# Trainium2: moving head-projection units, output products, output stores and the final scaling in an eight-core hybrid conv/attention layer

## Chip, cores and metric

One Trainium2 chip (trn2), all 8 cores, each with its own share of the work and no traffic between them. The metric is device time in microseconds of the slowest core, from one launch.

## What is computed

```python
def hybrid_layer(x, ...):                       # x: (2, 4096, 4096) fp32
    proj = einsum('bsd,de->bse', rmsnorm(x, g_in), w_in)
    gB, gC, h, z_conv, c_q, c_kv, k_rope, z_attn = split(proj)   # 4x2048, 1024, 512, 64, 2048
    y_conv = gB * causal_short_conv(gC * h, conv_w) * silu(z_conv)
    q = rmsnorm(c_q) @ w_uq                     # 16 heads x (128 + 64 rotary)
    k_nope, v = split(rmsnorm(c_kv) @ w_ukv)    # 16 heads x (128 + 128)
    attn = chunk_causal_attention(rope(q), rope(k), v)           # chunks of 64 frames
    y = concat(y_conv, attn * silu(z_attn))
    return x + y @ w_out
out = rmsnorm(hybrid_layer(...), g_final)
```

## The kernel before

Each core owns 1024 query tokens (16 chunks of 64) of one sequence and computes everything for them; for the keys it projects all 4096 tokens of the sequence. All operands of TensorE are bf16. The program is written out instruction by instruction; `Prog` finds dependences from the addresses touched and turns them into semaphore waits. Every engine (PE, ACT, DVE, POOL, SP) runs its list strictly in the order written. At the end (`finish`, L163) each of the five engines waits for the last event of all engines and for every outstanding DMA. SP issues nearly all DMAs; POOL issues the ones that convert fp32 to bf16.

Stages in order of time:

- Convolution group (L429 to L672): projections in tiles of 128 channels; the last product of each tile f is stored to DRAM (`ysp`, L671).
- Latent keys (L756 to L792): 32 token tiles T. `post(T)` (L711) normalises and applies the rotary tables `cst` and the gain `gkv`, which SP loads at L756 to L758, behind the last `ysp` store.
- Query latents (L804): squares by ACT, summed over channels with a product with ones, which `pend` puts into the middle of the next tile (L813, L818).
- Attention (L1008): 16 heads h, each with query block b=0 (8 steps i of 256 keys) and b=1 (16 steps). A step issues the QK products of the next step (L946, L947), the exponential of its own (ACT, L1026), then perhaps one unit of projection work for the next head (Q: L882, K: L891, V: L900), the mask (DVE, L1045) and the products with V (L1052); DVE adds the exponentials up one step behind (L1059). The step's width is 512 queries; in the last 8 steps of a block it narrows from 512 to 64. `SKIP` names steps that take no unit. A unit needs a PSUM bank (`ubank`: bank 6 or 7) and is copied out in the next step, Q by DVE, K and V by ACT. A V unit covers 512 keys for two heads, so head 15's V comes with head 14's.
- Head 15 has no next head. It takes 8 pieces (`early`, four matmuls each) of the first output tile's product (L1001); the convolution results `YCV` and the weights `WO` for it are loaded when head 14's units are done (L1018 to L1022).
- Output (L1108): two groups g of four 128-token tiles, each 8 column tiles ct of 512, each 8 weight blocks kg (`WO`, 512 KB each, ten buffers, the load of block i+10 issued after block i's products). `evac` (L1087) adds the residual `XR` on DVE and squares on ACT. After group 0's last column tile `finish_tile` (L1094) scales all four tiles on DVE, 16 pieces of 1024 columns, and stores each; group 1 reuses the same `H` buffers. Group 1's last column tile is done tile by tile, with `finish_tile` after each.

Of the kernel before, what the change touches and what calls it, by code (L numbers as in the profile page):

```python
# [11 lines left out]
ALU = mybir.AluOpType  # L12
# [11 lines left out]
DMA_SEMS = {"sp": 40, "pool": 24}  # L24
# [60 lines left out]
class Prog:  # L85
# [77 lines left out]
    def finish(self):  # L163
# [6 lines left out]
        for e in ENGS:  # L170
            i = Ins(e, len(self.ins[e]), None, 0)
            i.deps = [x for x in evs if not (x.eng == e and x.dma_sem is None)]
            self.ins[e].append(i)
            self.order.append(i)
        known = {e: {} for e in ENGS}
        for ins in self.order:
            kn = known[ins.eng]
            todo = sorted(ins.deps, key=lambda x: -x.idx)
            for d in todo:
# [10 lines left out]
                kn[key] = val  # L190
            ins.known = dict(kn)
# [79 lines left out]
def build_program():  # L271
# [30 lines left out]
    with stack:  # L302
# [316 lines left out]

        wt = 2 * NF  # L620
# [183 lines left out]
        for m in range(8):  # L804
            w = WS[(64 + m) % 2]
            for hf in range(2):
# [142 lines left out]
        def finish_block(h, b_):  # L949
# [23 lines left out]
            [Z_Q + j * 4 * KB for j in range(4)] + [Z_R + 8 * KB, Z_R + 12 * KB, Z_R, Z_K2, Z_K2 + 4 * KB, Z_R + 4 * KB])]  # L973
# [8 lines left out]
        def woload(i):  # L982
# [7 lines left out]
            [Z_R + (16 + 2 * j) * KB for j in range(4)] + [Z_RB + 16 * KB + 512 + 2 * j * KB for j in range(4)])]  # L990
# [13 lines left out]
        SKIP = {(1, 1), (1, 3), (1, 5), (1, 7)}  # L1004
        qk(0)
        behind, slow, done = [], [], []
        us = []
        for n in range(len(steps)):  # L1008
            h, b_, i, off, w = geom(n)
            if b_ == 0 and i == 0:  # L1010
                us = []
                if h < 15:
                    us = units_of(h + 1)
                    pr = h // 2 + 1
                    if pr < 8:
                        us += [lambda s_=s_, pr=pr: unit_v(pr, s_) for s_ in range(8 * (h % 2), 8 * (h % 2) + 8)]
                else:
                    for i_ in range(6):  # L1018
                        woload(i_)
                    for f in range(16):  # L1020
                        dma("sp", YCV[:, f, :], ysp[f], [], [YCV[:, f, :], {("dr", "y", f)}])
                    load("sp", GF[:, :], gfin_d)  # L1022
# [5 lines left out]
            if us and (b_, i) not in SKIP:  # L1028
                us.pop(0)()
            if n % 6 == 0:  # L1030
                wcast(n // 6)
            if h == 15:
                pbanks[:] = [6]
                m_ = n - 360
                if m_ == 18:
                    woload(6)
                if 5 <= m_ < 9:
                    early.append((0, m_ - 5, 3))
                elif 14 <= m_ < 22 and m_ % 2 == 0:
                    early.append((0, m_ // 2 - 7, 2))  # L1040
                if early and early[-1] not in done:
                    done.append(early[-1])
                    out_mm(*early[-1][:2], early[-1][2], early[-1][1])
# [42 lines left out]

        def evac(g, ct, t_):  # L1087
            j = 32 * g + 4 * ct + t_
            h_ = H[t_][:, ct * 512:(ct + 1) * 512]
            tt(h_, bank(obank(ct, t_ + 4 * g)), XR[j % 8][:, :], ALU.add)  # L1090
            act(jk[:, :], h_, AF.Square, accum=fst[4 * g + t_][:, ct:ct + 1])  # L1091
            load_res(j + 8)

        def finish_tile(t_, pieces):  # L1094
            f_ = fst[t_]
            P.add("dve", lambda e: e.reduce_sum(out=f_[:, 8:9], in_=f_[:, 0:8], axis=AX.X), [f_[:, 0:8]], [f_[:, 8:9]])
            act(f_[:, 9:10], f_[:, 8:9], AF.Sqrt, scale=1.0 / D, bias=EPSA)
            recip(f_[:, 10:11], f_[:, 9:10])
            h_ = H[t_ % 4]
            n = D // pieces  # L1100
# [141 lines left out]
```

How the kernel before makes its waits and increments, by code:

```python
        def run(ename, eng):  # L207
            for i in self.ins[ename]:
                best = {}
                for d in i.waits:
                    key = d.dma_sem if d.dma_sem is not None else d.eng
                    val = d.dma_val if d.dma_sem is not None else d.ordinal
                    best[key] = max(best.get(key, 0), val)
                for key, val in best.items():
                    eng.wait_ge(dsem[key] if isinstance(key, tuple) else esem[key], val)
                if i.fn is None:
                    continue
                with nc.source_location(__file__, i.line):
                    r = i.fn(eng)
                if i.dma_sem is not None:
                    r.then_inc(dsem[i.dma_sem], 16)
                elif i.signal:
                    r.then_inc(esem[ename], 1)
```

The softmax here doesn't subtract the row's maximum and nothing guards it: scores larger than these inputs give would overflow.

## Time and profile before

| | |
|---|---|
| runs, us | 3679.06, 2735.65, 2737.66; median 2737.66 |
| profiled execution, us | 2735.57 |
| its span (slowest core, first to last instruction), us | 2734.0 |
| PE busy, us | 2671.2 (98% of the span) |
| DVE, ACT, POOL busy, us | 1419.5, 762.5, 79.2 |

Spans of all cores lie between 2726.2 and 2734.0 us. All views are of the slowest core, times in us from the start of its span. The profile shows a matmul from its start to a modelled end, so matmuls in a row overlap, and a short wait can vanish under the tail of the matmul before it.

### The profile page before, as it was taken

The page shows a single profiled execution, that of the slowest core. Times are in us where ns is not written, and L with a number is a line of the kernel's source. Part 1 is how long each engine was busy: PE and PEld are TensorE (multiplying, and loading weights), DVE is VectorE, ACT ScalarE, POOL GpSimd, SP SyncE. Part 2 cuts the span into 40 slices and gives each one's busy share as a digit, 9 for nine tenths or more (in the row PEclk, how much of TensorE's full clock was granted, in tenths as well). Part 3 has the DMA queues.
Part 4 walks back from the last instruction along what each step waited for, and adds up shares of the span by engine and source line. Part 5 has one row for each costly group of instructions (what it writes and reads, how often), then busy time and mean ns, then how long its engine had stood idle before and what let it go on. Part 6 is the DMA issues. An engine that isn't in the chain of part 4 may idle for free.

```text
span 2734.0 us, 41718 instructions; the slowest of 8 cores (2726.2 to 2734.0 us)
## 1 busy us (share of the span) xinstructions
PE 2671.2 (98%) x15646; PEld 1414.7 (52%) x15646; DVE 1419.5 (52%) x2314; ACT 762.5 (28%) x1187; POOL 79.2 (3%) x151
## 2 busy tenths in 40 slices
PE   6999999999999999999999999999999999998996
PEld 3446655555555555554444555555656544443443
DVE  3766765555555446664554257767676772013013
ACT  2300000000000026640110267666666661011011
POOL 0000000000000001100000000000000000000000
PEclk8999999999999999999999999999999999999998
DMA  9836666666666618855455544455435846568664
GB/s 216 206 103 161 162 170 174 169 171 178 180 171 167 133 32 138 134 134 160 125 176 152 101 72 56 71 78 70 63 47 78 101 147 213 187 187 247 230 194 167
DMA packets 122102, 390.87 MB, mean 143 GB/s; under 512 B 13616, under 2 KB 17968, under 8 KB 121776
## 3 DMA queue, kind: packets, MB, share of 16 engines
q1 hardware_dynamic: 97920, 308.24, 39.2%
q0 software_dynamic: 23984, 79.96, 20.1%
q8 instruction: 128, 2.10, 0.3%
q14 instruction: 70, 0.57, 0.1%
HBM read 447.13 MB, written 54.53 MB: 183 GB/s over the span
## 4 chain that ended last, share of the span: by engine, by line
PE 92%; DMA 3%; DVE 3%; issue 1%; ACT 1%; SPq 0%; DVEq 0%; ACTq 0%; POOLq 0%
PE ps L594 27%; PE ps L1001 14%; PE ps L832 8%; PE ps L702 7%; PE ps L1052 4%; PE ps L947 4%; PE ps L946 4%; PE ps L900 4%; PE ps L891 4%; PE ps L882 4%; PE ps L545 4%; PE ps L812 3%; PE ps L526 2%; PE ps L703 1%; DMA ust_90<-w_in_t 1%
## 5 line engine op out<-in xcount | busy, mean ns | idle before, releaser
L594 PE MATMUL ps<-XG,ws_67 128*128 128x384 bf16 (+2 forms) x2176 | 371.5, 332 | 0.0
L594 PE MATMUL ps<-XG,ws_66 128*128 128x384 bf16 (+2 forms) x2176 | 371.5, 332 | 0.0
L594 PEld LDWEIGHTS ps<-XG,ws_66 128*128 128x128 bf16 x2176 | 212.9, 98 | 154.5
L594 PEld LDWEIGHTS ps<-XG,ws_67 128*128 128x128 bf16 x2176 | 212.9, 98 | 154.3
L946 PE MATMUL ps<-QN_153,KH_149 128*128 128x512 bf16 (+7 forms) x384 | 115.2, 317 | 0.0
L946 PE MATMUL ps<-QN_154,KH_150 128*128 128x512 bf16 (+7 forms) x384 | 115.2, 317 | 0.0
L947 PE MATMUL ps<-TQ_156,K_61 128*128 128x512 bf16 (+7 forms) x384 | 115.2, 317 | 0.0
L947 PE MATMUL ps<-TQ_155,K_61 128*128 128x512 bf16 (+7 forms) x384 | 115.2, 317 | 0.0
L667 ACT ACTIVATE CC<-UU,convw 128x1024 f32<-128x1024 f32 x16 | 18.4, 1151 | 336.0 <-DVE UU L663 336.0
L832 PE MATMUL ps<-XG,ws_66 128*128 128x512 bf16 x512 | 112.0, 379 | 0.0
L832 PE MATMUL ps<-XG,ws_67 128*128 128x512 bf16 x512 | 111.8, 379 | 0.0
L1026 ACT ACTIVATE PT_157<-ps 128x1024 bf16<-128x1024 f32 x96 | 84.6, 882 | 66.4 <-PE ps L947 66.4
L1091 ACT ACTIVATE jk<-H_182 128x512 bf16<-128x512 f32 x16 | 10.1, 630 | 321.5 <-DVE H_182 L1090 321.5
L1090 DVE TENSOR_TENSOR H_182<-ps,XR_191 128x512 f32<-128x512 f32 x8 | 5.5, 692 | 168.5 <-PE ps L1001 168.5
L409 DVE TENSOR_TENSOR ws_66<-stg_70,g_in 128x1024 bf16<-128x1024 f32 x51 | 62.2, 1220 | 51.4 <-DMA stg_70<-w_in_t 51.4
L409 DVE TENSOR_TENSOR ws_67<-stg_70,g_in 128x1024 bf16<-128x1024 f32 x50 | 61.1, 1221 | 48.2 <-DMA stg_70<-w_in_t 48.0
L409 DVE TENSOR_TENSOR ws_67<-stg_68,g_in 128x1024 bf16<-128x1024 f32 x51 | 62.3, 1221 | 45.9 <-DMA stg_68<-w_in_t 45.8
L1026 ACT ACTIVATE PT_159<-ps 128x768 bf16<-128x768 f32 (+1 forms) x96 | 70.9, 739 | 54.1 <-PE ps L947 53.1
L409 DVE TENSOR_TENSOR ws_67<-stg_69,g_in 128x1024 bf16<-128x1024 f32 x51 | 62.3, 1221 | 44.3 <-DMA stg_69<-w_in_t 44.3
L1090 DVE TENSOR_TENSOR H_182<-ps,XR_187 128x512 f32<-128x512 f32 x8 | 5.5, 691 | 150.8 <-PE ps L1001 150.8
L409 DVE TENSOR_TENSOR ws_66<-stg_68,g_in 128x1024 bf16<-128x1024 f32 x51 | 62.2, 1220 | 40.0 <-DMA stg_68<-w_in_t 40.0
L409 DVE TENSOR_TENSOR ws_66<-stg_69,g_in 128x1024 bf16<-128x1024 f32 x50 | 61.0, 1221 | 40.4 <-DMA stg_69<-w_in_t 40.4
(503 smaller groups left out, 4804.3 us busy)
## 6 DMA issues: line engine op xcount, KB each, us to landing
stg_68<-w_in_t SPq DMA_DIRECT2D x102, 512.0 KB, 5.9
stg_69<-w_in_t SPq DMA_DIRECT2D x101, 512.0 KB, 6.1
stg_70<-w_in_t SPq DMA_DIRECT2D x101, 512.0 KB, 6.1
wbf<-w_out_t POOLq DMA_DIRECT2D x64, 512.0 KB, 18.9
wst<-w_ckv SPq DMA_DIRECT2D x16, 576.0 KB, 5.4
XG<-x_own POOLq DMA_DIRECT2D x7, 1024.0 KB, 20.3
WO_172<-wbf SPq DMA_DIRECT2D x13, 512.0 KB, 3.8
WO_173<-wbf SPq DMA_DIRECT2D x13, 512.0 KB, 4.3
```

The lines of the kernel that those rows point to most:

```text
L409: tt(WS[i % 2][:, 8 * c:8 * c + 8, :], stg[q % 3][:, :, :], gains(8, 8 * c, 128), ALU.mult)
L545: mm(bank(nb[0] % 8), uw[(u + g) % 8][:, kc - k0, :], XG[:, kc, 512 * hf:512 * hf + 512], kc == k_start, kc == k_end - 1)
L594: mm(o, w[:, kc, :], XG[:, kc, c0:c1], kc == 0, kc == 31)
L702: mm(psum[:, A, :], x_, WC[:, kc, 0:512], kc == 0, kc == 31)
L832: mm(o, w[:, kc, :], XG[:, kc, c0:c0 + 512], kc == 0, kc == 31)
L882: mm(o, WQ[h % 2][:, kc, part * 128:(part + 1) * 128], CQG[:, kc, bi * 512:(bi + 1) * 512], kc == 0, kc == 7)
L891: mm(o, w[:, kc, (h % 2) * 128:(h % 2) * 128 + 128], CKVN[:, kc, s_ * 512:(s_ + 1) * 512], kc == 0, kc == 3)
L900: mm(o[:, t_ * 256:(t_ + 1) * 256], CKVN[:, kc, c0:c0 + 128], w[:, kc, 256:512], kc == 0, kc == 3)
L946: mm(o, KH[h % 2][:, k0:k0 + 128], QN[h % 2][:, c0:c0 + w], True, False)
L947: mm(o, K2[:, k0:k0 + 128], TQ[h % 2][:, c0:c0 + w], False, True)
L1001: mm(bank(obank(ct, t_)), src[:, kc % 16, t_ * 128:(t_ + 1) * 128], WO[slot][:, kcc, :], kc == 0, kc == 31)
L1026: act(pt[:, :, 0:w], psum[:, 2 * (n % 2):2 * (n % 2) + 2, 0:w], AF.Exp, scale=ATTN_SCALE)
```

## The change

1. `finish`: only SP waits for the final events, and waits of one instruction are sorted oldest first.
2. `gkv`, the first four `cst` and one Sqrt on ACT move from the start of the latent stage into the last convolution tile (f = 15).
3. The ones-product of the query latents is issued one half tile later.
4. Heads 13 to 15: V units 8 to 15 of the last pair move from head 13 to head 14; head 13's block 1 takes units in steps 8, 10, 12, 14 only; head 14's order is V, K, Q; 12 early output pieces (6 of token tile 3, 6 of token tile 2), the first in head 14; the loads for them move to steps 7 and 11 of head 14's block 1, and from step 7 on units have bank 6 only. `WO` and `XR` buffers swap places to allow it.
5. Group 0's 16 scaled pieces (`scaled`) are issued one per two weight blocks in group 1.
6. In group 1 `evac` multiplies by the gain `GF` at once (DVE); the sum of squares of the first seven column tiles is taken early; at the end `scaled_fast` multiplies by the row's factor alone: half the columns on DVE, half on ACT, which issues its own stores.

```diff
             i = Ins(e, len(self.ins[e]), None, 0)
-            i.deps = [x for x in evs if not (x.eng == e and x.dma_sem is None)]
+            i.deps = [x for x in evs if e == "sp"]
...
+            ins.waits.sort(key=lambda x: x.idx)
...
+                if f == 15:
+                    act(stat[0][:, 7:8], EPSA, AF.Sqrt)
+                    load("sp", gkv[:, :], g_kv_d)
+                    for T in range(4):
+                        load_cs(T)
...
-                    if kc == 15 and pend:
+                    if kc == 15 and len(pend) > 1:
...
+        SKIP = {12: {(1, 1), (1, 3), (1, 5), (1, 7)},
+                13: {(1, i) for i in (0, 1, 2, 3, 4, 5, 6, 7, 9, 11, 13, 15)}, 14: set()}
+        EARLY = dict(zip((-3, 0, 3, 5, 6, 7), [(kg, 3) for kg in range(6)]))
+        EARLY.update(zip((13, 15, 16, 17, 19, 21), [(kg, 2) for kg in range(6)]))
...
+                    if h == 14:
+                        us = [lambda s_=s_: unit_v(7, s_) for s_ in range(8, 16)] + us[4:] + us[:4]
...
+            if h == 14 and b_ == 1:
+                if i == 7:
+                    pbanks[:] = [6]
+                    for f in range(16):
+                        if f in (0, 4):
+                            woload(f // 4)
+                        dma("sp", YCV[:, f, :], ysp[f], [], [YCV[:, f, :], {("dr", "y", f)}])
+                if i == 11:
+                    for i_ in range(2, 6):
+                        woload(i_)
...
             act(jk[:, :], h_, AF.Square, accum=f_[:, ct:ct + 1])
+            if later:
+                later.pop(0)()
+            if g == 1:
+                later.append(lambda: tt(h_, h_, GF[:, ct * 512:(ct + 1) * 512], ALU.mult))
...
+            elif ct == 7:
+                act(f_[:, 9:10], f_[:, 7:8], AF.Sqrt, scale=1.0 / D, bias=f_[:, 8:9])
+                while later:
+                    later.pop(0)()
+                recip(f_[:, 10:11], f_[:, 9:10])
...
+        def scaled_fast(t_):
+            r_ = fst[t_][:, 10:11]
+            n = 1024 if t_ < 7 else 512
+            for c in range(0, 2048, n):
+                lo = H[t_ % 4][:, c:c + n]
+                ts(lo, lo, r_, ALU.mult)
+                dma("sp", out[t_ * 128:(t_ + 1) * 128, c:c + n], lo, [lo], [])
+            for c in (2048, 3072):
+                hi = H[t_ % 4][:, c:c + 1024]
+                act(hi, hi, AF.Copy, scale=r_)
+                dma("act", out[t_ * 128:(t_ + 1) * 128, c:c + 1024], hi, [hi], [])
...
                     woload(i0 + kg + NW)
+                    if outs and kg % 2 == 0:
+                        scaled(*outs.pop(0))
...
-                for t_ in range(4):
-                    finish_tile(t_, 4)
+                outs = [(t_, c, c + 1024) for c in range(0, D, 1024) for t_ in range(4)]
```

How the order changes, at three places. On PE, head 13, block 1, from the unit of step 8 to the products with V (`VH`) of step 10; `QN` with `KH` and `TQ` with `K` are the QK products. Before:

```order
L900 MATMUL ps<-WKV_164,CKVN 128x256 x8
L1052 MATMUL ps<-PT_157,VH_151 128x512 x2
L946 MATMUL ps<-QN_154,KH_150 128x384
L947 MATMUL ps<-TQ_156,K_61 128x384
L946 MATMUL ps<-QN_154,KH_150 128x384
L947 MATMUL ps<-TQ_156,K_61 128x384
L900 MATMUL ps<-WKV_164,CKVN 128x256 x8
L1052 MATMUL ps<-PT_158,VH_151 128x448 x2
```

After:

```order
L895 MATMUL ps<-CKVN,WKV_164 128x512 x4
L1062 MATMUL ps<-PT_157,VH_151 128x512 x2
L950 MATMUL ps<-QN_154,KH_150 128x384
L951 MATMUL ps<-TQ_156,K_61 128x384
L950 MATMUL ps<-QN_154,KH_150 128x384
L951 MATMUL ps<-TQ_156,K_61 128x384
L1062 MATMUL ps<-PT_158,VH_151 128x448 x2
```

The V units (L900) are gone from this head; a K unit stands in every second narrow step, and steps 0 to 7 of the block have none.

On SP, where group 0 ends: residual tiles, then stores and weight blocks. Before:

```order
L360 DMA XR_194<-xres 128x512
L1104 DMA out<-H_182 128x1024 x4
L1104 DMA out<-H_183 128x1024 x4
L1104 DMA out<-H_184 128x1024 x4
L1104 DMA out<-H_185 128x1024 x4
L360 DMA WO_176<-wbf 128x2048
```

After:

```order
L361 DMA XR_194<-xres 128x512
L361 DMA WO_176<-wbf 128x2048
L1123 DMA out<-H_182 128x1024
L361 DMA WO_177<-wbf 128x2048
L361 DMA WO_178<-wbf 128x2048
L1123 DMA out<-H_183 128x1024
```

The weight load no longer stands behind 16 stores; a store follows every second load.

On DVE, the last token tile (`H_185`). Before:

```order
L1090 TENSOR_TENSOR H_185<-ps,XR_194 128x512
L1096 TENSOR_REDUCE fst_202<-fst_202 128x1
L350 RECIPROCAL fst_202<-fst_202 128x1
L1103 SCALAR_TENSOR_TENSOR H_185<-H_185,fst_202,GF 128x512 x8
```

After:

```order
L1103 TENSOR_TENSOR H_185<-ps,XR_194 128x512
L1108 TENSOR_TENSOR H_185<-H_185,GF 128x512
L351 RECIPROCAL fst_202<-fst_202 128x1
L1131 TENSOR_SCALAR H_185<-H_185,fst_202 128x512
L1131 TENSOR_SCALAR H_185<-H_185,fst_202 128x512 x3
```

Four scalings instead of eight remain on DVE; the other half of the columns is on ACT (two Copy of 1024 columns, each followed by a store).

## Rows read from the trace of the kernel before

**Rows 1.** The page, busy time of the engines, and PE in 40 slices (tenths).
```profile
PE 2671.2 (98%) x15646; PEld 1414.7 (52%) x15646; DVE 1419.5 (52%) x2314; ACT 762.5 (28%) x1187; POOL 79.2 (3%) x151
...
PE   6999999999999999999999999999999999998996
```
**Rows 2.** Who PE waited for: us in total, times, longest.
```profile
PE ps L1001 <- DMA WO_176<-wbf: 7.7, 1, 7.7
...
PE ps L703 <- DVE t_0_141 L731: 2.3, 1, 2.3
PE ps L1052 <- DVE PT_157 L1045: 2.2, 5, 0.8
PE ps L1052 <- DVE PT_159 L1045: 1.8, 4, 0.6
...
PE ps L818 <- ACT sq_0_145 L817: 1.2, 2, 0.6
```
**Rows 3.** Timeline of SP's issues, group switch: start, us, what.
```profile
2506.29 3.92 SPq L1104 DMA_DIRECT2D out<-H_185  x4
2510.30 0.40 SPq L360 DMA_DIRECT2D WO_176<-wbf  x1
```
**Rows 4.** Timeline of PE, same place: start, us, what, idle before.
```profile
2524.70 5.48 PE L1001 MATMUL ps<-WO_176,YCV 128*128 128x512 bf16 x16 [7.66 <-DMA WO_176<-wbf]
```
**Rows 5.** Output stage by windows: busy us (count) per engine, PE clock, DMA share, GB/s.
```profile
2300.00:2400.00 100.00, 100.00 (x465) 45.36 (x464) 8.62 (x14) 9.39 (x26) 0.00 (x0) 1.00 0.59 186
...
2500.00:2525.00 25.00, 17.34 (x80) 7.68 (x79) 11.76 (x14) 3.18 (x9) 0.00 (x0) 0.93 1.02 271
2525.00:2550.00 25.00, 25.00 (x109) 11.03 (x108) 2.58 (x4) 2.17 (x6) 0.00 (x0) 0.93 0.94 310
```
**Rows 6.** Windows of head 14's narrow steps and head 15, same columns.
```profile
2224.40:2233.60 9.20, 6.95 (x48) 3.64 (x47) 7.90 (x16) 5.08 (x8) 0.00 (x0) 1.00 0.97 264
2233.60:2245.40 11.80, 9.90 (x64) 4.96 (x63) 9.35 (x22) 6.71 (x11) 0.00 (x0) 1.00 1.04 356
2245.40:2258.70 13.30, 12.86 (x61) 5.59 (x60) 10.84 (x12) 8.56 (x11) 0.00 (x0) 1.00 0.25 86
2258.70:2267.80 9.10, 8.25 (x57) 4.72 (x56) 7.76 (x16) 5.13 (x8) 0.00 (x0) 1.00 0.04 16
```
**Rows 7.** Timeline of DVE, head 15, wide steps without a unit.
```profile
2251.32 1.23 DVE L1059 TENSOR_TENSOR ACC_166<-ACC_166,PT_160 128x1024 f32<-128x1024 f32 x1 [0.17 <-DVE ACC_166 L1059]
...
2253.90 0.69 DVE L968 TENSOR_TENSOR rl<-rl,G 128x512 f32<-128x512 f32 x1
```
**Rows 8.** Chain of waits where the latent stage begins: start, us, what.
```profile
950.89 10.89 DMA cst_130<-cs_key
```
**Rows 9.** Timeline of the end.
```profile
2712.18 1.03 PE L1001 MATMUL ps<-WO_179,G 128*128 128x512 bf16 x4
2714.65 0.68 DVE L1090 TENSOR_TENSOR H_185<-ps,XR_194 128x512 f32<-128x512 f32 x1
...
2717.17 5.39 DVE L1103 SCALAR_TENSOR_TENSOR H_185<-H_185,fst_202,GF 128x512 f32<-128x512 f32 x8
2718.01 4.98 SPq L1104 DMA_DIRECT2D out<-H_185  x8
```
**Rows 10.** DMA issues of the end: count, KB each, median us to landing.
```profile
out<-H_185 SPq DMA_DIRECT2D x8, 256.0 KB, 3.8
```
**Rows 11.** Semaphore waits after 2723 us: count, ns, first and last start.
```profile
L215 SPq EVENT_SEMAPHORE  x20: 17/17/17, 2726.3 to 2727.2; - x20
```
**Rows 12.** Instructions of L302, the program's last line: count, ns, start.
```profile
L302 SPq DRAIN  x1: 7/7/7, 2727.3 to 2727.3; - x1
...
L302 POOLq DRAIN  x1: 6272/6272/6272, 2727.5 to 2727.5; - x1
```
**Rows 13.** Groups by line on the page: a 1024-column scaling on ACT (busy us, mean ns).
```profile
L667 ACT ACTIVATE CC<-UU,convw 128x1024 f32<-128x1024 f32 x16 | 18.4, 1151 | 336.0 <-DVE UU L663 336.0
```
**Rows 14.** DVE groups by line and form: a scaling by a per-row factor.
```profile
L655 DVE TENSOR_SCALAR WC<-wst,g_in 128x576 bf16<-128x576 f32 x32 | 15.1, 516 | 47.8 <-DMA wst<-w_ckv 47.8
```

More of the change, by code:

```diff
@@ L618, in prep, with load_cs @@
             tt(o[:, :], q[:, 0:256], q[:, 256:512], ALU.add)
+        pa = region(Z_RB + 8704, Z_RB + 16 * KB + 512)
+        gkv = pa("gkv", [512])
+        cst = [pa("cst%d" % i, [128]) for i in range(4)]
+        def load_cs(T):
+            if T < 32:
+                load("sp", cst[T % 4][:, :], cs_key[T])
         wt = 2 * NF
@@ L972, in build_program @@
         WO = [sb("WO%d" % i, o, [4, 512], BF16) for i, o in enumerate(
-            [Z_Q + j * 4 * KB for j in range(4)] + [Z_R + 8 * KB, Z_R + 12 * KB, Z_R, Z_K2, Z_K2 + 4 * KB, Z_R + 4 * KB])]
+            [Z_R + 16 * KB, Z_R + 20 * KB] + [Z_Q + j * 4 * KB for j in range(4)] + [Z_R, Z_K2, Z_K2 + 4 * KB, Z_R + 4 * KB])]
         NW = len(WO)
@@ L989, in build_program @@
         XR = [sb("XR%d" % i, o, [512]) for i, o in enumerate(
-            [Z_R + (16 + 2 * j) * KB for j in range(4)] + [Z_RB + 16 * KB + 512 + 2 * j * KB for j in range(4)])]
+            [Z_R + (8 + 2 * j) * KB for j in range(4)] + [Z_RB + 16 * KB + 512 + 2 * j * KB for j in range(4)])]
         fst = [sb("fst%d" % i, Z_T + 4 * KB + 64 * i, [12]) for i in range(8)]
@@ L1014, in build_program @@
                     pr = h // 2 + 1
-                    if pr < 8:
+                    if pr < 8 and h < 13:
                         us += [lambda s_=s_, pr=pr: unit_v(pr, s_) for s_ in range(8 * (h % 2), 8 * (h % 2) + 8)]
[L1017 to L1022, printed above, removed]
+                    if h == 14:
+                        us = [lambda s_=s_: unit_v(7, s_) for s_ in range(8, 16)] + us[4:] + us[:4]
             if n + 1 < len(steps):
@@ L1027, in build_program @@
             flush()
-            if us and (b_, i) not in SKIP:
+            if us and (b_, i) not in SKIP[min(max(h, 12), 14)]:
                 us.pop(0)()
+            if h == 14 and b_ == 1:
[8 more added lines that the diff above has]
+                        woload(i_)
+            if (h, b_, i) == (15, 0, 2):
+                load("sp", GF[:, :], gfin_d)
             if n % 6 == 0:
                 wcast(n // 6)
[L1032 to L1043, printed above, removed]
+            m_ = n - 360
+            if m_ == 18:
+                woload(6)
+            if m_ in EARLY:
+                kg, t_ = EARLY[m_]
+                early.append((0, kg, t_))
+                out_mm(0, kg, t_, kg)
             if i >= 8 * b_:
@@ L1085, in load_res @@
                 load("sp", XR[j % 8][:, :], xres[4 * g + t_, ct])
+        later = []
         def evac(g, ct, t_):
@@ L1089, in evac @@
             h_ = H[t_][:, ct * 512:(ct + 1) * 512]
+            f_ = fst[4 * g + t_]
             tt(h_, bank(obank(ct, t_ + 4 * g)), XR[j % 8][:, :], ALU.add)
-            act(jk[:, :], h_, AF.Square, accum=fst[4 * g + t_][:, ct:ct + 1])
-            load_res(j + 8)
[L1094 to L1100, printed above, removed]
-            for p in range(pieces):
-                c = slice(p * n, p * n + n)
-                stt(h_[:, c], h_[:, c], f_[:, 10:11], GF[:, c], ALU.mult, ALU.mult)
-                dma("sp", out[t_ * 128:(t_ + 1) * 128, c], h_[:, c], [h_[:, c]], [])
+            act(jk[:, :], h_, AF.Square, accum=f_[:, ct:ct + 1])
@@ new lines, in evac @@
+            if later:
+                later.pop(0)()
+            if g == 1:
+                later.append(lambda: tt(h_, h_, GF[:, ct * 512:(ct + 1) * 512], ALU.mult))
+            load_res(j + 8)
+            if ct == 6:
+                P.add("dve", lambda e: e.reduce_sum(out=f_[:, 8:9], in_=f_[:, 0:7], axis=AX.X), [f_[:, 0:7]], [f_[:, 8:9]])
+                ts(f_[:, 8:9], f_[:, 8:9], 1.0 / D, ALU.mult, EPS, ALU.add)
+            elif ct == 7:
[3 more added lines that the diff above has]
+                recip(f_[:, 10:11], f_[:, 9:10])
```

21 lines of the change are left out of this document (8 added, 13 removed).

## The prediction

> **What bounds the kernel now.** First the page: PE is busy 2671.2 of 2734.0 us, the other engines half the time or less, and in 40 slices PE falls under nine tenths only in the first slice (six tenths, some 25 us) and near the end [rows 1]. So a change of order can win only what PE idles, 62.8 us, of which the start is untouched, plus waits too short to show, plus whatever runs after the last matmul. Next, who PE waited for: one wait of 7.7 us for a weight block, one of 2.3 us in the latent stage, a dozen short ones in attention, two in the query latents [rows 2]. Next the timelines at these places, and last the end. The unit of all estimates is the 512-column matmul: 465 in 100 us, 0.215 us each [rows 5]. A step of width 512 without a unit is six of them, 1.29 us; a Q unit is eight, 1.72 us; a K or V unit and an early piece count as four, 0.86 us.
>
> **Group switch.** SP issues group 0's 16 stores before the next weight load, and each store waits for DVE's scaling: the last four take from 2506.29 to 2510.21, and only then goes WO_176 [rows 3], which lands 14 us later, since the stores fill the DMA engines (share 1.02) [rows 5]. PE idles 7.66 us, and the 16 matmuls behind the wait take 5.48 us instead of 16 x 0.215 + 0.16 = 3.6 us [rows 4]; the mean granted clock of this stretch is 0.93 [rows 5], so after the idle PE ran for a while at the lower of its two levels (1.2 GHz). Together 9.6 us. In the new order the load goes first and one store follows every second load, so no load waits behind more than one store; ten blocks are loaded ahead, 10 x 3.45 = 34 us. I take the whole 9.6 us; at the least 6, should a first block still come late. DVE's 16 scalings move into group 1, where it is nearly idle (8.62 us in 100 [rows 5]); group 1's `evac` must now wait until the pieces of its columns have landed, but PE then works in the other four banks for 27.6 us, which covers a store of some microseconds.
>
> **Latent stage.** The tables land 10.89 us after an issue that stood behind the last convolution store [rows 8], and PE waits 2.3 us for what needs them [rows 2]. Issued a tile earlier they land under convolution products, and so does the table switch of the Sqrt. Gain 2.3 us (1.5 to 2.6). The later ones-product removes the two waits of 1.2 us [rows 2]: 1.2 us (0.5 to 1.4), since half a tile, 3.4 us of products, then covers ACT's square.
>
> **Heads 13 to 15.** From head 14's step 8 to the last step PE idles 2.25 + 1.90 + 0.44 + 0.85 = 5.4 us [rows 6]. The nine largest waits average 0.44 us [rows 2], so there are about twelve, and each hides up to 0.16 us more: a matmul is shown for 1.03 - 3 x 0.215 = 0.38 us [rows 9] and the next starts after 0.215. That makes 7.4 us. Eight of these 32 steps have filling now, sixteen will. I take three quarters, 5.5 us (3 to 7). Against it stand three costs, none of which the old trace shows directly.
> - Head 13's steps 0 to 7 lose their units. PE then needs 8 x 1.29 + 2 x 0.215 = 10.8 us; DVE needs 8 adds of 1.23 + 0.17 us and four operations of 0.69 us for the sums of the block before, 14.0 us [rows 7]. The mask of step 8 stands behind these adds on DVE, and the products with V behind the mask. At most 3.2 us; at least 0, since in head 15, where six of the eight wide steps already have no unit, PE idles only 0.44 us in all of them [rows 6]. I take 1.5.
> - With bank 6 alone each Q unit waits until DVE has copied out the one before: 0.69 us behind the rest of an add, while PE has 2 x 0.215 plus four narrower products, about 1.1 us, to do. Three times 0 to 1 us: 1.5.
> - The weights of the third early piece are queued behind 18 transfers (5.8 MB). At 356 GB/s [rows 6] they need 16 us and some 3 us to land; PE gets there after about 20 us of steps and units. 0.5 (0 to 4).
>
> Net gain 2.0 us (-7 to +7).
>
> **The end.** The last matmul ends at 2712.18 + 1.03 = 2713.2; DVE takes up the last tile only at 2714.65, because it still scales the tile before, and starts scaling 2.52 us later [rows 9]. In the new order every tile costs DVE two scalings instead of four, so it is free: the tile starts at 2713.35, and scaling, with the same chain of square, root and reciprocal (the product with `GF` lies beside ACT's square and root), at 2715.95. Before, eight stores were issued from 2718.01 to 2722.99 [rows 9], each landing a median 3.8 us later [rows 10], the last at 2726.3, where the final waits begin [rows 11]. Now ACT sets the end: 1.15 us a half [rows 13], an issue of 0.4 us as on SP [rows 3], again 1.15, with 0.1 for each semaphore: last issue 2718.85, landed 2722.65, gain 3.65 us. DVE's four take 516 x 512/576 = 0.46 us each [rows 14], done earlier; at 0.67 (5.39/8 [rows 9]) also. The other end of the range: if the transfers themselves set the pace, the tile needs the 8.3 us that it took from first issue to last landing, from 2716.45 to 2724.75, gain 1.55. I take 3.0, nearer to the measured time from an issue to its landing. The Trainium skill, DMA: Bandwidth & Descriptors, section "Issuing engines are not separate DMA queues", speaks for the lower end: stores issued on ACT interleave on the same 16 engines, and a second issuer saves only issue time. By that rule the gain here would be 1.55 and the total 1.5 us less.
>
> After 2726.3 every engine goes through 20 waits in turn (SP's last at 2727.2 [rows 11]); then POOL alone runs a DRAIN of 6.27 us, from 2727.5 [rows 12], and the program closes at 2734.0. With the waits on SP alone, POOL reaches its DRAIN after its last DMA issue, in head 15, where nobody waits for it. SP, oldest first, has a few waits left after the last landing: I allow 0.5 us, gain 7.2 (1.2 if the DRAIN comes last all the same). The end together: 10.2 us.
>
> **Sum.** 9.6 + 2.3 + 1.2 + 2.0 + 10.2 = 25.3 us, against the profiled execution of 2735.57 us (1.57 more than its span): 2710.3, forecast 2710. That execution lies 2.1 us under the median of the runs shown, 2737.66, and beside the lowest, 2735.65; I predict for a run like it.
>
> **Rivals.**
> - The DRAIN stays last, because POOL closes the program for all. For it: POOL's is the only long one [rows 12]. Against it: POOL began it only after its own waits. Time 2710 + 6 = 2716.
> - DVE becomes the bound in heads 13 and 14, with the refilled steps at the lower end of their gain, 3, and the three costs at 3.2, 3 and 2: net -5 instead of +2, 2717. For it: 14.0 against 10.8 us. Against it: the 0.44 us of head 15.
> - Slower than before: group 0's stores turn the DMA engines into the bound of group 1. Its first four column tiles then move 4 x (8 x 0.52 + 4 x 0.26 + 4 x 0.52) = 29.4 MB in 110.3 us, 266 GB/s. With stores alone the engines were full at 271 GB/s, with loads behind them at 310 (share 0.94) [rows 5], so the demand lies just under the rate. The 34 us loaded ahead move the point at which PE waits to 29.4 MB in 144.8 us, 203 GB/s; below 173 GB/s the wait exceeds 25.3 us and the kernel is slower. At half of 310, 155 GB/s, it would wait 45 us: 2755. The Trainium skill, HBM Reference, section "Specifications (TRN2)", puts a core's effective share at about 358 GB/s; by that, an estimate, 29.4 MB need 82 us and nothing waits. Rows 5 stay under that figure, but far above 173.
>
> **Chances.** Forecast 0.77 (2703 to 2717 with its bounds), DRAIN last 0.08, DVE the bound 0.12, DMA the bound 0.03. Range 2702 to 2721: the lower end has all terms at their better ends but one, the upper holds both middle rivals and small shortfalls together. About 2%, 55 us, is what a measurement of this kernel can tell from no change. To be faster by that, more than all reachable idle would have to go: 0.01. Slower by 2% is the tail of the last rival: 0.02. Within 2%: 0.97.
>
> **What would show it.** Right: no wait for `WO` at the group switch and a clock of 1.00 there; no wait at the first latent tiles; POOL's DRAIN before 2300 us and an end under 1 us after the last landing; under 3 us of idle from head 14's step 8 on. Wrong: idle in head 13's block 1, or waits for Q's copies in head 14's steps 9 to 11 (heads term); a DMA share at 1.0 over group 1's first half with waits for `WO` (DMA term); a last landing later than 11.5 us after the last matmul (end term).

## The result, and the profile after

In some executions, of either kernel, the granted clock of one die or of a pair of cores lies lower and the time is longer by 20 us to several hundred; all times, medians and ratios below leave these out.

| | kernel before | changed kernel |
|---|---|---|
| first runs | 2735.65, 2737.66 us | 2714.74 (profiled), 2717.26, 2718.00 us |
| ratio | 1 | 0.9927 [0.9898, 0.9956] |
| ten executions later, beside before's | median 2737.8 us | median 2718.0 us (2714.58 to 2719.96), 0.9928 |
| profiled execution | 2735.57 us, span 2734.0 | 2714.74 us, span 2713.2 |
| last matmul ends | 2713.2 us | 2699.0 us |
| last store lands, after the last matmul | 13.1 us (12.6 to 14.0 over the cores) | 13.7 us (10.2 to 15.0) |
| span ends, after the last matmul | 20.8 us | 14.2 us |

Some 20 us were won, 0.7%, within the 2% band and inside the stated range; the forecast of 2710 lies 5 us below the profiled execution and 8 below the median of the ten.

The page and the waits of PE, changed kernel:

```profile
PE 2671.6 (98%) x15646; PEld 1414.8 (52%) x15646; DVE 1425.9 (53%) x2344; ACT 772.1 (28%) x1196; POOL 79.3 (3%) x151
...
PE   6999999999999999999999999999999999999997
```

```profile
PE ps L1062 <- DVE PT_157 L1055: 0.9, 2, 0.5
PE ps L1062 <- DVE PT_160 L1055: 0.6, 1, 0.6
PE ps L1062 <- DVE PT_159 L1055: 0.4, 1, 0.4
```

The wait for `WO`, the one at the first latent tile and those for the square are gone [rows 2]; what is left below the start is a handful of attention waits. Windows of head 14's narrow steps, the next 12 us, head 15's wide and its narrow steps, and the group switch, columns as in [rows 5] (busy us and count of PE, PEld, DVE, ACT, POOL, then PE clock, DMA share, GB/s):

```profile
2224.00:2233.00 9.00, 8.34 (x55) 4.53 (x56) 6.24 (x13) 2.78 (x6) 0.00 (x0) 1.00 0.94 333
2233.00:2245.00 12.00, 11.28 (x72) 5.66 (x70) 9.84 (x23) 6.79 (x11) 0.00 (x0) 1.00 0.85 315
2245.00:2258.00 13.00, 13.00 (x62) 5.76 (x61) 10.87 (x14) 9.08 (x10) 0.00 (x0) 1.00 0.25 83
2258.00:2267.00 9.00, 8.37 (x59) 4.83 (x58) 7.29 (x16) 4.18 (x7) 0.00 (x0) 1.00 0.00 0
...
2500.00:2525.00 25.00, 25.00 (x117) 11.37 (x116) 9.26 (x11) 2.89 (x8) 0.00 (x0) 1.00 0.87 282
2525.00:2550.00 25.00, 25.00 (x118) 11.33 (x116) 9.76 (x12) 2.89 (x8) 0.00 (x0) 1.00 0.87 277
```

PE idles 0.66 + 0.72 + 0 + 0.63 = 2.0 us in the first four, against 5.4 [rows 6]. At the group switch PE is full, at a clock of 1.00 instead of 0.93 [rows 5], and the DMA engines are at 0.87: no bound. SP's timeline there shows one store among the loads, where sixteen stood:

```profile
2502.23 0.32 SPq L361 DMA_DIRECT2D WO_172<-wbf  x1
2502.64 0.38 SPq L1123 DMA_DIRECT2D out<-H_185  x1
2505.68 0.32 SPq L361 DMA_DIRECT2D WO_173<-wbf  x1
```

The end, as a timeline (the counterpart of [rows 9]), then the median times from issue to landing of its stores:

```profile
2697.97 1.03 PE L1005 MATMUL ps<-WO_179,G 128*128 128x512 bf16 x4
...
2699.10 0.69 DVE L1103 TENSOR_TENSOR H_185<-ps,XR_194 128x512 f32<-128x512 f32 x1 [2.94 <-PE ps L1005]
...
2701.64 1.15 ACT L1135 ACTIVATE H_185<-H_185,fst_202 128x1024 f32<-128x1024 f32 x1 [0.64 <-DVE fst_202 L351]
2701.65 1.67 DVE L1131 TENSOR_SCALAR H_185<-H_185,fst_202 128x512 f32<-128x512 f32 x4
...
2704.47 0.34 ACTq L1136 DMA_DIRECT2D out<-H_185  x1
```

```profile
out<-H_185 SPq DMA_DIRECT2D x4, 256.0 KB, 8.4
out<-H_185 ACTq DMA_DIRECT2D x2, 512.0 KB, 7.3
```

The issuing side came as foreseen: scaling starts 2.6 us after the last matmul and the last issue stands 5.5 us after it (before: 9.4 to 9.8). But on this core a store now takes 7 to 8 us to land, not 3.8 [rows 10], so the last landing is no earlier than before. It lies 13.7 us after the last matmul, and a landing later than 11.5 was the prediction's own sign of a wrong end term. And behind it:

```profile
L303 POOLq DRAIN  x1: 61334/61334/61334, 2121.3 to 2121.3; - x1
...
L303 SPq DRAIN  x1: 7/7/7, 2713.0 to 2713.0; - x1
```

POOL's DRAIN [rows 12] lies 530 us before the end, and the span closes 0.5 us after the last landing.

To weigh the stages on all cores I summed PE's gaps: from one matmul's start to the next, less its columns at 0.215 us per 512 (cores with missing matmul records left out).

| PE gaps, us | first 100 us | latent stages | heads 13 to 15 | output stage |
|---|---|---|---|---|
| before, slowest core (1) | 34.4 | 15.4 | 9.1 | 10.3 |
| before, other cores | 32.2 to 35.9 | 12.7 to 13.6 | 9.1 | 6.4 to 11.9 |
| changed, slowest core (3) | 37.8 | 11.4 | 5.6 | 0.6 |
| changed, other cores | 32.8 to 34.4 | 11.4 | 5.6 | 0.6 |

On the slowest cores: 9.7 (output) + 4.1 (latents) + 3.5 (heads) - 3.4 (start) + 0.3 = 14.2 us at the last matmul (the 0.3 from earlier heads), and 20.8 - 14.2 = 6.6 us behind it: 20.8 us in all.

### The profile page after: what moved, and what is told of

It is laid out like the page before. It is cut to its first block, busy times and chain, and to the rows that moved or that the text cites. A ratio compares the mean times of both kernels' runs of the same rounds, so it can differ in the third digit from the quotient of the medians.

```text
span 2713.2 us, 41751 instructions; the slowest of 8 cores (2707.0 to 2713.2 us)
## 1 busy us (share of the span) xinstructions
PE 2671.6 (98%) x15646; PEld 1414.8 (52%) x15646; DVE 1425.9 (53%) x2344; ACT 772.1 (28%) x1196; POOL 79.3 (3%) x151
## 4 chain that ended last, share of the span: by engine, by line
PE 97%; DMA 2%; SPq 0%; ACT 0%; issue 0%; DVE 0%; ACTq 0%; DVEq 0%; POOLq 0%
PE ps L595 27%; PE ps L1005 16%; PE ps L709 8%; PE ps L836 8%; PE ps L1062 4%; PE ps L951 4%; PE ps L950 4%; PE ps L904 4%; PE ps L895 4%; PE ps L816 4%; PE ps L886 4%; PE ps L546 4%; PE ps L527 2%; PE ps L710 1%; DMA ust_90<-w_in_t 1%; DMA XG<-x_own 1%
## 5 line engine op out<-in xcount | busy, mean ns | idle before, releaser
L595 PEld LDWEIGHTS ps<-XG,ws_66 128*128 128x128 bf16 x2176 | 212.9, 98 | 154.5
L595 PEld LDWEIGHTS ps<-XG,ws_67 128*128 128x128 bf16 x2176 | 212.9, 98 | 154.4
L410 DVE TENSOR_TENSOR ws_66<-stg_70,g_in 128x1024 bf16<-128x1024 f32 x51 | 62.2, 1220 | 39.7 <-DMA stg_70<-w_in_t 39.7
L410 DVE TENSOR_TENSOR ws_67<-stg_69,g_in 128x1024 bf16<-128x1024 f32 x51 | 62.2, 1220 | 38.6 <-DMA stg_69<-w_in_t 38.6
L410 DVE TENSOR_TENSOR ws_67<-stg_68,g_in 128x1024 bf16<-128x1024 f32 x51 | 62.3, 1221 | 37.4 <-DMA stg_68<-w_in_t 37.4
L1029 ACT ACTIVATE PT_158<-ps 128x896 bf16<-128x896 f32 (+1 forms) x96 | 77.2, 804 | 16.1 <-PE ps L951 15.9
L836 PEld LDWEIGHTS ps<-XG,ws_66 128*128 128x128 bf16 x512 | 50.2, 98 | 60.3
L836 PEld LDWEIGHTS ps<-XG,ws_67 128*128 128x128 bf16 x512 | 50.0, 98 | 60.5
```

The lines of the kernel that those rows point to most:

```text
L410: tt(WS[i % 2][:, 8 * c:8 * c + 8, :], stg[q % 3][:, :, :], gains(8, 8 * c, 128), ALU.mult)
L595: mm(o, w[:, kc, :], XG[:, kc, c0:c1], kc == 0, kc == 31)
L1029: act(pt[:, :, 0:w], psum[:, 2 * (n % 2):2 * (n % 2) + 2, 0:w], AF.Exp, scale=ATTN_SCALE)
```

## The experiments

First the parts of the change alone or undone, then the end. Each is told with the median of its executions and their number; the landing is the last store's, counted from the last matmul's end, over the eight cores of the profiled execution.

**The final waits alone.** The kernel before, with

```diff
-            i.deps = [x for x in evs if not (x.eng == e and x.dma_sem is None)]
+            i.deps = [x for x in evs if e == "sp"]
...
+            ins.waits.sort(key=lambda x: x.idx)
```

> The kernel before with one part of the change: only SP waits for the last events, oldest first. Theory of the prediction: POOL's DRAIN runs as soon as POOL has issued its last DMA, long before the end, and the span ends 0.5 us after the last landing: 7.2 us less than before, some 2728.4 by the profiled execution, last matmul to end of the span 13.6 instead of 20.8 us. Rival (the DRAIN comes last whatever waits): POOL's DRAIN still ends the span, at most 1.2 us less, some 2734. The landing of the last store is left at 13.1 us after the last matmul by both.

Measured 2728.4 us (6 executions; the kernel before had 2736.4 beside it), the span ending 12.3 to 14.2 us after the last matmul, 0.3 us after the last landing. The profile has the DRAIN early, at full length:

```profile
L303 POOLq DRAIN  x1: 58929/58929/58929, 2122.3 to 2122.3; - x1
```

The rival is out: some 7 to 8 us of the change come from these two edits, which were not taken apart.

**The spread stores alone.** The kernel before, with group 0's pieces dealt as in the changed kernel.

```diff
...
+                    if outs and kg % 2 == 0:
+                        scaled(*outs.pop(0))
...
-                    finish_tile(t_, 4)
+                    root(t_)
+                outs = [(t_, c, c + 1024) for c in range(0, D, 1024) for t_ in range(4)]
```

> The kernel before with one part of the change: group 0's scalings and stores are dealt over group 1's first four column tiles; the tail is as before. Theory of the prediction: the 7.7 us wait for the weight block at the group switch and the lower clock behind it go, 9.6 us less, some 2726, the granted clock of the switch 1.00, DMA share of group 1's first half under 0.95. Rival (the stores only move the wait to a later weight load): waits for weight blocks of several us between 2510 and 2630, less than 5 us gained.

Measured 2726.1 us (4 executions); PE's gaps in the output stage 0.6 us on every core with whole records, from 6.4 to 11.9; the windows of the switch:

```profile
2500.00:2525.00 25.00, 24.84 (x115) 11.31 (x117) 7.45 (x8) 2.89 (x8) 0.00 (x0) 1.00 0.92 245
2525.00:2550.00 25.00, 24.89 (x115) 11.32 (x116) 7.36 (x8) 2.89 (x8) 0.00 (x0) 1.00 0.89 256
```

The wait did not move to a later load.

**Heads put back.** The changed kernel without the new `SKIP`, `EARLY`, order of units, places of `WO` and `XR`, and loads of `YCV`.

> The changed kernel with the order of heads 13 to 15 put back (units, early pieces, the places of the weight and residual buffers, the loads of the convolution outputs); all else as changed. The prediction's term was 2.0 us, so this kernel would be 2.0 us slower than the changed one; by PE's gaps in the two traces (9.2 us of stalls in these heads before, 5.7 after) it should be 3.5 to 4.4 us slower, about 2718.5. Rival (the gain is given back as a later wait, the refilled steps only move it): within 1 us of the changed kernel.

Measured 2720.0 us (6 executions, 2718.1 to 2722.9), 2 us over the changed kernel's 2718.0, which was measured in another series. Against the kernel before of each series (2736.4 and 2737.8) it is 3.4 us. The gaps, which don't hang on the landing, are 8.75 us on each of cores 1, 4, 5 and 7 instead of 5.62: 3.1 us. The gain is real, and larger than the 2.0 forecast.

**Latent stage put back.**

```diff
-                if f == 15:
-                    act(stat[0][:, 7:8], EPSA, AF.Sqrt)
-                    load("sp", gkv[:, :], g_kv_d)
-                    for T in range(4):
-                        load_cs(T)
...
+        load("sp", gkv[:, :], g_kv_d)
+        for T in range(4):
+            load_cs(T)
...
-                    if kc == 15 and len(pend) > 1:
+                    if kc == 15 and pend:
```

> The changed kernel with the latent stage put back (the tables and the vector loaded after the gated convolution, the first ones-product not put off); all else as changed. Theory of the prediction: the waits of 2.3 us and twice 0.6 us come back, 3.5 us slower than the changed kernel, some 2718. Rival (the stage is held by something else and the wait only moved): under 1 us.

The gaps in the latent stages come back at 12.4 to 16.8 us over the cores, from 11.36 on each, so 1 to 5 us. The time does not show it: 2716.0 us (7 executions). Core 1, with the longest latent wait, happened to land first (10.4 us), and others at 16 us; the time, a maximum over eight cores, can hide a loss that differs from core to core.

**The end: is the last tile behind the three before it?**

```diff
-                        scaled_fast(4 + t_)
+                        if t_ == 3:
+                            scaled_fast(4 + t_)
```

> The changed kernel, which leaves out the scaling and the stores of the three token tiles 4 to 6: only the last tile (7) is scaled and stored at the end. Theory A (backlog: the 8.4 MB of four tiles go out in the last 27 us as fast as the transfers allow, and the last tile's stores stand behind those of tile 6): with the queue empty the last tile's stores land 3 to 5 us after issue, the last landing is 9 to 10 us after the last matmul instead of 13.7, on all cores alike. Theory B (the last tile's own 2 MB or the interleaving of the two issuers sets it): the landing stays at 11 to 14 us.

Measured landings of 9.7 to 14.1 us, equal within half a microsecond on two neighbouring cores (9.7 and 9.8 on cores 4 and 5, 14.1 twice on 6 and 7), and 2712.0 us (3). One pair agrees with A, one with B: a backlog is part of it, not all.

**The end: the old scaling.**

```diff
-            if g == 1:
-                later.append(lambda: tt(h_, h_, GF[:, ct * 512:(ct + 1) * 512], ALU.mult))
...
-                        scaled_fast(4 + t_)
+                        for c in range(0, D, 1024 if t_ < 3 else 512):
+                            scaled(4 + t_, c, c + (1024 if t_ < 3 else 512))
```

> The changed kernel with the last four tiles scaled as before: four or eight fused scalings on DVE alone, all stores from SP; the final waits, the spread stores and the heads as changed. Theory A (backlog of transfers): issues come about 3 us later, but the last landing is within 1.5 us of the changed kernel's 13.7 us after the last matmul (spread of 10 to 15 over the cores), the time within 1.5 us. Theory B (issue sets the end, as the prediction had it): the last landing 3 us later than with two engines, the time 3 us longer.

Measured 2712.6 us (4; 0.9906 [0.9886, 0.9925]), faster than the changed kernel (2718.0 in another series; the kernels before had 2738.9 and 2737.8), with the last issue at 8.25 us and landings of 12.2 to 14.5 us. So the two-engine end as it was built is a loss, by more than theory A allowed.

**The end: tiles further apart.** Two blocks of column tile 6 are kept for the token tiles; the ten blocks that `WO` holds suffice.

```diff
                     for t_ in range(4):
+                        for kg in (6, 7):
+                            out_mm(6, kg, 4 + t_, (i0 - 8 + kg) % NW)
+                        evac(g, 6, t_)
                         for kg in range(8):
...
-                for kg in range(8):
+                for kg in range(6 if (g, ct) == (1, 6) else 8):
...
```

> The changed kernel with another order of the last products: the last two weight blocks of column tile 6 are also taken token tile by token tile, so that each of the last four tiles has 40 products of four matmuls, 8.6 us, instead of 32, 6.9 us, and the stores of tiles 4 to 6 start 5.2, 3.4 and 1.7 us earlier against the last matmul. Theory A (backlog): 2 MB per 8.6 us is 244 GB/s, under the rate of the stores, so the last tile's stores find the queue nearly empty: last landing 9.5 to 11 us after the last matmul, 2 to 4 us less on the slowest core, some 2711. Theory B: no change of the landing (13.7 us after the last matmul), the time within 1 us. A third way: the last blocks come later than the products that now need them sooner, with a wait of 1 to 5 us at the first tile.

Measured 2716.2 us (4), landings 10.9 and 11.5 on cores 0 and 1, but 16.5 to 17.0 on the other six. Theory A holds on one pair of cores and fell on the others: with 244 GB/s of demand their engines still fell behind.

**Issuer against supply.** The next four ran beside each other, the changed kernel itself among them.

> The changed kernel once more, as the measure for the three beside it: 2714 to 2718 us; last landing 10 to 15 us after the last matmul, the same within 1 us on the two cores 2k and 2k+1 and several us apart from pair to pair; on every core 5.6 us of PE gaps in heads 13 to 15 and 0.6 in the output stage.

> The changed kernel with the second half's stores of the last four tiles issued from SP, not from ACT; the scaling stays on both engines. Theory Q (two issuers' stores interleave on the same 16 DMA engines, and that lowers what the engines move): with one issuer the landings fall back to the range of the kernels with SP alone, 12 to 14.5 us after the last matmul or below, none over 15, the DMA engines moving over 300 GB/s when they are full. Theory S (the faster scaling supplies the 2 MB of a tile within 2.3 us on all cores at once, and the memory that neighbouring cores share is the limit): no change, 10 to 17 us, 180 to 300 GB/s at a full share.

> The last four tiles scaled as before, on DVE alone (the supply of the kernel before), but every second piece's store issued from ACT. Theory Q: the landings spread to 15 us and more after the last matmul on some pairs of cores, 2 to 4 us later than with SP alone. Theory S: as with SP alone, 12 to 14.5 us, the time 2711 to 2715.

> The last tiles scaled on DVE alone and stored from SP, and the last two weight blocks of column tile 6 taken token tile by token tile, so that the tiles end 8.6 us apart instead of 6.9. Theory Q: with one issuer the engines keep up with 244 GB/s, the last landing follows the last issue (8.25 us after the last matmul) by 3 to 4 us: 11.5 to 12.5 us on all cores, the time 2709 to 2712. Theory S: supply is slow here too, so the same. Neither (the shared memory is slower than 244 GB/s a core): 14 to 17 us as in the other kernel with this order.

The edits: `dma("act", ...)` to `dma("sp", ...)` in `scaled_fast`; the old scaling with every second piece issued from ACT; the old scaling from SP with the tiles further apart. The changed kernel, windows around the last matmul (2696.3) on its slowest core and the times from issue to landing of its stores, then the one with SP alone (2696.2):

```profile
2685.00:2693.00 8.00, 8.00 (x39) 3.61 (x38) 3.86 (x8) 4.28 (x6) 0.00 (x0) 1.00 0.96 221
2693.00:2701.00 8.00, 3.30 (x16) 1.26 (x13) 3.59 (x8) 3.94 (x7) 0.00 (x0) 0.90 1.03 202
2701.00:2708.00 7.00, 0.00 (x0) 0.00 (x0) 0.00 (x0) 0.70 (x1) 0.00 (x0) 0.50 1.05 225
...
out<-H ACTq DMA_DIRECT2D x3, 512.0 KB, 11.6
out<-H SPq DMA_DIRECT2D x4, 256.0 KB, 12.8
```

```profile
2685.00:2693.00 8.00, 7.95 (x38) 3.64 (x38) 3.96 (x7) 4.30 (x7) 0.00 (x0) 1.00 1.01 281
2693.00:2701.00 8.00, 3.17 (x15) 1.26 (x13) 3.47 (x8) 4.29 (x7) 0.00 (x0) 0.89 1.03 278
2701.00:2708.00 7.00, 0.00 (x0) 0.00 (x0) 0.00 (x0) 0.00 (x0) 0.00 (x0) 0.50 0.99 298
...
out<-H SPq DMA_DIRECT2D x4, 256.0 KB, 6.6
```

At the same full share (next to last number) the engines move 202 to 225 GB/s in the one and 278 to 298 in the other: same bytes, same supply. Theory S fell. The changed kernel itself landed at 17.7 to 19.6 us, later than the 10 to 15 expected from its first profile, where the same stores on the slowest core (last matmul at 2699.0) still had

```profile
2688.00:2696.00 8.00, 8.00 (x38) 3.62 (x37) 3.97 (x7) 4.29 (x6) 0.00 (x0) 1.00 1.01 275
2696.00:2702.00 6.00, 2.99 (x14) 1.16 (x12) 1.97 (x5) 2.53 (x5) 0.00 (x0) 1.00 1.04 316
```

So the lower rate is not there in every execution. Two issuers with the old scaling lost nothing either (landings of 11.8 to 14.8 us, against Theory Q), and neither theory had said why. The old scaling from SP with the tiles further apart landed at 12.5 to 14.1 us, later than the 11.5 to 12.5 expected, since its last issue came at 9.2 us and not at 8.25. One thing had been changed unseen with the issuer. SP alone sends a tile's columns in rising order, while the changed kernel sends quarters 1, 3, 2, 4, so that stores to places 8 KB apart in a row are under way together.

**Order of the columns against issuer.**

> The changed kernel with all stores of the last tiles from SP, and the tiles 8.6 us apart instead of 6.9 (the last two weight blocks of column tile 6 taken token tile by token tile). Theory Q (two issuers with a backlog lower what the engines move; with SP alone they keep 260 to 300 GB/s): 244 GB/s of demand leave no backlog, the last landing follows the last issue (5.9 us after the last matmul) by about 4 us: 9.5 to 11.5 us, the time 2708 to 2711, under both kernels. Theory S (the memory is the limit whatever the issuer): as the kernel with this order and two issuers, 14 to 17 us, 2714 to 2717.

> The changed kernel with all stores of the last tiles from SP, in the order in which two issuers would send them: a piece of the first half of the columns, one of the second, and so on. Theory Q1 (what costs is that two issuers have stores outstanding at once): as with SP alone, 11.5 to 14.5 us from the last matmul to the last landing, the time 2711 to 2713. Theory Q2 (what costs is writing columns 8 KB apart by turns, whoever issues): 16 to 19 us, 2715 to 2720.

> The same mixed order with all stores of the last tiles issued from ACT, none from SP. Theory Q1 (two issuers at once): as with SP alone, 11.5 to 15 us from the last matmul to the last landing. Theory Q3 (stores issued from ACT are slower in themselves): 16 to 20 us, the engines at a full share moving 215 to 250 GB/s.

The mixed order, all from SP (all from ACT in the third), lies in the loop:

```diff
-            for c in range(0, 2048, n):
+            for k in range(2):
+                for c in range(1024 * k, 1024 * k + 1024, n):
...
-            for c in (2048, 3072):
+                c = 2048 + 1024 * k
...
```

Windows of the mixed order from SP (last matmul at 2694.9), then SP in rising order with the tiles 8.6 us apart (2695.0), each with its last stores:

```profile
2685.00:2693.00 8.00, 8.00 (x38) 3.63 (x37) 3.06 (x6) 4.16 (x6) 0.00 (x0) 1.00 1.03 191
2693.00:2701.00 8.00, 1.93 (x9) 0.69 (x7) 3.13 (x7) 3.20 (x5) 0.00 (x0) 0.87 1.07 215
```

```profile
out<-H SPq DMA_DIRECT2D x4, 256.0 KB, 14.2
out<-H SPq DMA_DIRECT2D x2, 512.0 KB, 14.6
```

```profile
2685.00:2693.00 8.00, 8.00 (x39) 3.63 (x37) 4.38 (x9) 3.87 (x7) 0.00 (x0) 1.00 0.87 240
2693.00:2701.00 8.00, 1.96 (x10) 0.69 (x7) 3.73 (x8) 3.21 (x5) 0.00 (x0) 0.84 0.87 251
```

```profile
out<-H SPq DMA_DIRECT2D x4, 256.0 KB, 3.8
out<-H SPq DMA_DIRECT2D x2, 512.0 KB, 5.7
```

With one issuer and the mixed order the engines are full at 191 to 215 GB/s: the loss needs no second issuer (Q2). In rising order, with room between the tiles, they keep up at a share of 0.87; the last tile's 256 KB stores again take 3.8 us, and the 512 KB stores behind them 5.7. The ACT kernel says little: landings of 12.0 to 18.0 us and 2719.2 us (4), but ACT's stores and scalings wait for each other there, and on one core it issues as late as 14.2 us after the last matmul. Stores from ACT alone can land at 12.0 us, as on cores 6 and 7, so Q3 finds no support; and the mixed order was not slow on these two cores.

**Two issuers in column order.** The opposite test: both issuers stay, each engine takes alternate quarters.

```diff
-            for c in range(0, 2048, n):
+            for c in [b + d for b in (0, 2048) for d in range(0, 1024, n)]:
...
-            for c in (2048, 3072):
+            for c in (1024, 3072):
```

> The changed kernel, two issuers as in it, with the columns dealt otherwise: DVE scales the first and third quarter (stores from SP), ACT the second and fourth (stores from ACT), so that the pieces of a tile are issued in the order of the columns. Theory Q2 (what costs is a backlog of stores in which pieces 8 KB apart in a row alternate): the landings fall to 11.5 to 14.5 us after the last matmul, the time to 2711 to 2713, as with SP alone and columns in order. Theory Q1 (two issuers at once cost it as well): 15 to 19 us, 2715 to 2719, as the changed kernel.

> The same dealing of columns, two issuers, with the last tiles 8.6 us apart instead of 6.9. Theory Q2: no backlog and the last issue at 5.5 us: 10.5 to 12 us from the last matmul to the last landing, 2708 to 2710.5, no worse than the kernel with this order and SP alone (11.2 to 12.2 us). Theory Q1: 13 to 17 us, 2712 to 2717, as the first kernel with this order.

Landings 10.7 to 13.1 and 10.5 to 12.1 us, without a time that counts; both ran again:

> The changed kernel with two issuers and the columns of a tile issued in order, once more for its time: by its landings (10.7 to 13.1 us after the last matmul) Theory Q2 gives 2711 to 2713, Theory Q1 2715 to 2719.

> Two issuers, columns in order and the last tiles 8.6 us apart, once more for its time: by its landings (10.5 to 12.1 us after the last matmul) 2708 to 2710.5 under Theory Q2, level with the kernel that stores from SP alone in this order (2708.9 to 2710.1); 2712 to 2717 under Theory Q1.

Measured 2711.5 and 2710.9 us, landings 11.3 to 12.9 and 10.8 to 12.7: about level with SP alone. Q1 is out. The windows of the first of the two on its slowest core (last matmul at 2698.2):

```profile
2685.00:2693.00 8.00, 8.00 (x39) 3.63 (x37) 3.07 (x6) 4.03 (x7) 0.00 (x0) 1.00 0.93 273
2693.00:2701.00 8.00, 5.21 (x25) 2.14 (x22) 3.77 (x8) 3.75 (x7) 0.00 (x0) 1.00 0.97 322
```

All variants of the end in one table (spacing of the last tiles in us; n executions). The last column is the kernel before in the same series; it differs by 2.2 us between series, so smaller differences between rows of different series decide nothing.

| scaling, issuer, order of columns | spacing | landing, us | time, median us (n) | before, us |
|---|---|---|---|---|
| DVE, SP, rising | 6.9 | 12.2 to 14.5 | 2712.6 (4) | 2738.9 |
| DVE, both, rising | 6.9 | 11.8 to 14.8 | 2712.8 (4) | 2737.8 |
| both, SP, rising | 6.9 | 11.7 to 14.0 | 2711.6 (5) | 2737.8 |
| both, both, rising | 6.9 | 11.3 to 12.9 | 2711.5 (3) | 2739.0 |
| both, both, mixed (changed kernel) | 6.9 | 17.7 to 19.6 | 2718.0 (10) | 2737.8 |
| both, SP, mixed | 6.9 | 16.3 to 21.1 | 2718.8 (8) | 2736.8 |
| DVE, SP, rising | 8.6 | 12.5 to 14.1 | 2711.4 (4) | 2737.8 |
| both, both, mixed | 8.6 | 10.9 to 17.0 | 2716.2 (4) | 2738.9 |
| both, both, rising | 8.6 | 10.8 to 12.7 | 2710.9 (4) | 2739.0 |
| both, SP, rising | 8.6 | 11.2 to 12.2 | 2709.3 (4) | 2736.8 |

The last one beats both kernels: 0.9900 of the kernel before in its series, where the changed kernel had 0.9928 in its own, a difference of some 8 us.

## Why the prediction was right and where it was wrong

- **Group switch, 9.6 us: right.** (Its parts add up to 9.5.) 9.7 on the slowest core, and alone 2726.1 where 2726 was expected. No load came late, DMA share 0.87 to 0.92; the rival of a DMA-bound group 1 did not appear.
- **Latents, 2.3 + 1.2 us: right in kind.** Every core now has 11.4 us of gaps there. The gain is what the core lost before: 4.1 us on the slowest, 1.3 to 2.3 on the others. The time of the kernel with the stage put back does not show it.
- **Heads, 2.0 us net: mechanism right, size low.** 3.5 us. The costs set against the gain were over-sized. Head 13's gaps rose from 0.3 to 1.3 us, 1.0 where 1.5 was taken; head 14's Q units with one bank wait 0.5, taken as 1.5; the early piece's weights came in time, taken as 0.5. Heads 14 and 15 fell from 8.9 to 4.4 us with these 0.5 in it, so the refilled steps gave about 5.0, taken as 5.5. These parts are read from the gaps; no run took them apart. The rival with DVE as the bound is out.
- **The final waits, 7.2 us: right.** From last landing to end of span 20.8 - 13.1 = 7.7 us before, 0.5 now: 7.2. POOL reaches its DRAIN at 2121 us, over 100 us before head 15 and not in it, as the prediction had it; the term does not depend on that.
- **The stores, 3.0 us: wrong, and this is the step that failed:** "last issue 2718.85, landed 2722.65", which puts the last landing 3.8 us behind the last issue, and the choice of 3.0 as "nearer to the measured time from an issue to its landing". The issue was right: 5.5 us after the last matmul, forecast 5.65. The landing was not. On the slowest core the last tile's stores took 7.3 to 8.4 us (medians; landing 0.6 us later than before, a gain of -0.6), and 11.6 to 12.8 in the later profile of the same kernel (landings 17.7 to 19.6 us, some 5 us later than before). Two things are in this:
  - The 3.8 us belonged to stores that DVE alone released over 5 us [rows 9]. Released faster, they land later even in rising order: with two issuers the store that lands last took 5.8 to 8.2 us over the cores, with the DMA engines at shares of 0.93 to 0.97 in the windows above, where that of the kernel before took 3.2 to 4.5. The landings then lie at 11.3 to 12.9 us instead of 12.6 to 14.0, a gain of about 1 us. That is near the prediction's other end, 1.55 with the transfers setting the pace, and not near 3.0.
  - The mixed order costs the rest: some 7 us of time by the table, though less in the first profile. The lower end, "the tile needs the 8.3 us", left the pace of the transfers as it was, and did not look at where in a row the stores of two engines fall; so the gain of -0.6 lies below it too.
- **The Trainium skill's rule** (DMA: Bandwidth & Descriptors, "Issuing engines are not separate DMA queues") pointed to the lower side, rightly: in rising order a second issuer brings the last issue from 5.9 to 5.5 us and gains nothing measurable (2711.5 against 2711.6, in different series). It does not cover the loss, which one issuer shows as well.
- **The start**, left out of the sum as untouched, took 3.4 us more on the slowest core of the profiled execution. It differs by 4 to 5 us from core to core in the two profiles, and the slowest core is the one where it and the last landing fall badly together.

With 3.0 replaced by -0.6, heads by 3.5, latents by 4.1 and the start by -3.4 the sum is 9.7 + 4.1 + 3.5 - 0.6 + 7.2 - 3.4 + 0.3 = 20.8, the measured difference. That the total came within 5 us of the forecast is partly luck: the stores and the start took 7.0 us from the sum, while heads and latents, taken too small, gave 2.1 back.

## What to carry to other kernels

A time from issue to landing belongs to the pace and the order in which its stores were sent; do not carry it over when either changes. When work is dealt to two engines, check which addresses are then under way together, and deal columns so that they still go out in rising order. Room between the last tiles shows as 0.6 to 2.3 us in the table, with either order, which is hardly more than the series differ, and did not make up for the mixed one. Here the gains that every core had in full size (group switch, 5.8 us of gaps and more; heads, 3.5) showed in the time; the latent gain, small on most cores and large on one, did not.

## What the runs showed of the hardware

- With quarters of a row by turns full DMA engines moved 191 to 225 GB/s, from one issuer or two; in rising order 278 to 298 from one issuer, and 273 to 322 at shares of 0.93 to 0.97 from two. It is not so in every execution: the mixed order had 275 and 316 at a full share in the first profile of the changed kernel. The median time was some 7 us longer with the mixed order (2718.0 against 2711.5, 2718.8 against 2711.6). Why (memory, or the engines) no run here tells.
- Last landings of two neighbouring cores (2k, 2k+1) mostly lie within 1 us of each other, and at most 2, where pairs differ by up to 6; on cores 0 and 1 the mixed order reached 10.2 to 10.8 us in two kernels (the changed one, and with the latent stage put back). It fits a path that two cores share, which was not tested by itself.
- POOL's DRAIN is not of a fixed length: 6.27 us at the program's end, 53 to 64 us over cores and runs when POOL reaches it early. There it begins as the last weight copies are issued (2121.3 us) and ends at 2182.6, 3.1 to 3.2 us after the last of them lands.
